# Forget-gate attention: where the next head's decay sums and six half projections stand among a head's eight iterations

## The reference, cut to what matters

```python
log_f = jax.nn.log_sigmoid(f_logit + b_f)
f_cum = jnp.cumsum(log_f, axis=1).transpose(0, 2, 1)
...
logits = jnp.einsum("bhqd,bhkd->bhqk", qi, k) * scale
logits = logits + fi[..., :, None] - f_cum[..., None, :]
logits = jnp.where(pi[:, None] >= kpos[None, :], logits, -jnp.inf)
probs = jax.nn.softmax(logits, axis=-1)
return jnp.einsum("bhqk,bhkd->bhqd", probs, v)
...
return o * jax.nn.silu(z)
```

## Time and profile before

| what | us |
|---|---|
| median of 3 runs (lowest, highest) | 3028.71 (3024.96, 3031.01) |
| profiled execution, its own time | 3029.29 |
| its span, first to last instruction | 3028.0 |
| PE busy | 2837.0 |
| ACT busy | 1349.0 |
| DVE busy | 1617.8 |
| POOL busy | 856.2 |

### The profile page before, as it was taken

How to read it: one execution, slowest core, us unless ns; L and a number is a source line. 1 busy time by engine, 2 the same in 40 slices (tenths; PEclk the granted TensorE clock), 3 DMA queues, 4 the chain that set the end, 5 groups by cost and what they waited for, 6 DMA issues and landing times.

```text
span 3028.0 us, 36823 instructions
## 1 busy us (share of the span) xinstructions
PE 2837.0 (94%) x14072; PEld 2328.6 (77%) x14072; DVE 1617.8 (53%) x2879; ACT 1349.0 (45%) x2400; POOL 856.2 (28%) x671
## 2 busy tenths in 40 slices
PE   7989989998999999999997999999999999989987
PEld 6777768776778888887774777778888888877876
DVE  5656674543288888886587676630002434342034
ACT  5656773434266666674434334451113334332122
POOL 1333341223255544542111221123221111103331
PEclk9999999999999999999998999999999999999999
DMA  3011111221100000002351110012211010101231
GB/s 126 29 39 32 39 70 53 78 86 35 34 10 14 10 10 10 10 28 84 101 163 71 46 35 22 15 51 68 70 49 42 22 35 29 28 15 56 70 111 69
DMA packets 54445, 148.81 MB, mean 49 GB/s; under 512 B 6144, under 2 KB 14976, under 8 KB 54272
## 3 DMA queue, kind: packets, MB, share of 16 engines
q1 hardware_dynamic: 54272, 146.46, 15.1%
HBM read 129.66 MB, written 16.78 MB: 48 GB/s over the span
## 4 chain that ended last, share of the span: by engine, by line
PE 81%; DVE 9%; ACT 6%; issue 3%; DMA 1%; POOL 1%; SPq 0%; DVEq 0%; ACTq 0%; POOLq 0%
PE ps L317 75%; PE ps L362 4%; PE ps L659 1%; ACT t L302 1%; PE ps L2380 1%; DVE t L1019 1%; DVE t L1564 0%; ACT t L698 0%; POOL t L308 0%; DVE t L2617 0%; DVE t L1841 0%; DMA t<-in_abias 0%; DVE t L2624 0%; DVE t L2714 0%; DVE t L1743 0%
## 5 line engine op out<-in xcount | busy, mean ns | idle before, releaser
L317 PE MATMUL ps<-t,t 128*128 128x512 f32 (+7 forms) x12184 | 2668.8, 378 | 149.8 <-DVE t L758 27.3
L317 PEld LDWEIGHTS ps<-t,t 128*128 128x128 f32 (+3 forms) x12184 | 2123.9, 188 | 626.9 <-issue 110.5
L308 POOL TENSOR_TENSOR t<-t,t 128x1024 fp32r<-128x1024 f32 (+2 forms) x171 | 358.9, 2099 | 1320.7 <-ACT t L302 1320.1
L302 ACT ACTIVATE t<-t 128x1024 fp32r<-128x1024 f32 (+2 forms) x205 | 186.9, 912 | 698.1 <-PE ps L317 696.3
L1620 POOL TENSOR_SCALAR t<-t,t 128x1024 f32<-128x1024 f32 x128 | 145.2, 1135 | 183.0 <-DVE t L1570 180.0
L362 PE MATMUL ps<-t,t 128*128 128x128 f32 x1176 | 160.5, 274 | 13.4 <-DVE t L1564 7.7
L1564 DVE TENSOR_TENSOR t<-ps,t 128x512 fp32r<-128x512 f32 x256 | 164.2, 681 | 15.7 <-ACT t L1481 13.9
L362 PEld LDWEIGHTS ps<-t,t 128*128 128x128 f32 x1176 | 132.0, 140 | 37.6 <-issue 26.4
L1577 DVE TENSOR_REDUCE t<-ps 128x1 f32<-128x1024 f32 x128 | 154.0, 1203 | 2.0 <-PE ps L317 1.9
L1481 ACT ACTIVATE t<-ps 128x512 fp32r<-128x512 f32 x256 | 140.2, 592 | 11.5 <-PE ps L362 7.4
L1489 ACT ACTIVATE t<-ps,t 128x1024 f32<-128x1024 f32 x128 | 142.7, 1115 | 1.9 <-DVE t L1577 1.5
(11 more groups left out here) (217 smaller groups left out, 2427.2 us busy)
## 6 DMA issues: line engine op xcount, KB each, us to landing
t<-in_wflat SPq DMA_DIRECT2D x156, 512.0 KB, 3.6
t<-in_wada SPq DMA_DIRECT2D x48, 256.0 KB, 3.4
t<-in_xT SPq DMA_DIRECT2D x16, 512.0 KB, 8.1
t<-in_wflat SPq DMA_DIRECT2D x32, 128.0 KB, 2.0
hd<-t SPq DMA_DIRECT2D x8, 512.0 KB, 3.1
t<-hd SPq DMA_DIRECT2D x8, 512.0 KB, 7.5
x2d<-t SPq DMA_DIRECT2D x8, 512.0 KB, 4.0
md<-t SPq DMA_DIRECT2D x16, 256.0 KB, 4.3
```

Of the source, the lines that this page charges most:

```text
L302: ac.activation(whi[i % 2][:, 0:n], raw[i % 2][:, 0:n], ACT.Copy).then_inc(*on.up(ac, "whi", i))
L308: e.tensor_tensor(wlo[i % 2][:, 0:n], raw[i % 2][:, 0:n], whi[i % 2][:, 0:n], ALU.subtract) \
L317: return pe.matmul(o, l, r, start=start, stop=stop)
```

## The change

It puts the two decay sums first in `parts` and the six half projections behind them, and adapts the three places that turn a step's number into a half. On all three engines the steps of iterations 0 to 7 are then sum 0, sum 1, Q0, Q1, K0, K1, V0, V1, in place of Q0, Q1, K0, K1, V0, V1, sum 0, sum 1. The banks of the iterations, the sizes and everything else stay. In head 0's preparation the order changes in the same way.

```diff
@@ stage_attn_c
-            parts = [(FQ, 0), (FQ, 1), (FK, 0), (FK, 1), (FV, 0), (FV, 1), None, None]
+
+            parts = [None, None, (FQ, 0), (FQ, 1), (FK, 0), (FK, 1), (FV, 0), (FV, 1)]
@@ head(h, s, b), the branch of the sums
-                    hf = s - 6
+                    hf = s
                     bank["f", h, hf] = b
                     wait_bank(b)
@@ head_dv(h, s)
-                if s < 2:
-                    on.wait_ge(dv, "fq_hi", h, s)
-                    dv.scalar_tensor_tensor(Qf[h % 2][1][:, half(s)], ps[:, bank[FQ[h], s], :], C_SCALE, Qf[h % 2][0][:, half(s)], ALU.mult, ALU.subtract) \
-                        .then_inc(*on.up(dv, "fq_lo", h, s))
-                elif s < 4:
-                    hf = s - 2
+                hf = s % 2
+                if s in (2, 3):
+                    on.wait_ge(dv, "fq_hi", h, hf)
+                    dv.scalar_tensor_tensor(Qf[h % 2][1][:, half(hf)], ps[:, bank[FQ[h], hf], :], C_SCALE, Qf[h % 2][0][:, half(hf)], ALU.mult, ALU.subtract) \
+                        .then_inc(*on.up(dv, "fq_lo", h, hf))
+                elif s in (4, 5):
                     on.wait_ge(dv, "fk_hi", h, hf)
```

## The result

| | before | changed |
|---|---|---|
| median of 9 runs, us | 3028.71 | 3045.36 |
| lowest, highest | 3024.2, 3036.49 | 3036.03, 3052.99 |
| profiled execution: its time, span | 3029.29, 3028.0 | 3036.03, 3034.7 |
| first copy of z (start of the stage) to the end of the span | 849.1 | 861.2 |

The ratio is 1.0048, 95% interval 1.0032 to 1.0064: slower, by about 14.5 us, with 9.7 and 19.4 at the ends of the interval. The forecast was 3040, within 3034 to 3048.

The account below looks back on a forecast made before the run. The prediction took PE, busy 94% of the span, as the bound, so only gaps on PE count. Its terms, 16.0 + 0.5 + 0.7 - 6.1 = +11.1 us, gave a forecast of 3040 us, range 3034 to 3048.

Parts of the forecast that it names:

- Term 1: After the last V half, the chain to iteration 1's value products outlasts PE's remaining work: 1.67 us lost per head change.
- term 2: Between the transposes of iterations 1 and 2, a 3.13 us chain against 2.13 of PE work: 1.00 us lost per head change.
- term 4: Old stalls at iteration 7 (0.50 us, seven heads) and iteration 0 (0.44 us, six heads) go away: 6.1 us saved.
- Term 3, the loop's start: At the loop's start the first sum waits for V's half in bank 7, losing 1.48 us instead of 0.80: +0.7.
- Term 3, the last head: At the change to the last head the value products' wait loses 2.61 us instead of 2.13: +0.5.
- The clock did not fall at the six head changes: Rival: the clock falls to 1.2 GHz at all six head changes, up to 1.75 us each, giving 3050 us; 12%.
- No change: Rival: half of each loss at the head changes is hidden, giving 3032 us; 8%.
- Faster: Rival: the narrow iterations' chains are hidden and only the saving of old stalls remains, giving 3022.6 us; 4%.
- V's second half behind the first in bank 7: At the wide end V's second half waits for bank 7: expected free; as rival, about 1 us a head, 3047; 2%.

Follow-up runs that it names:

- free_banks: The changed kernel with the steps of iterations 0 and 1 writing banks 1 and 3 instead of 7 and 1; 3041.68 us, ratio 1.0044 to the kernel before.
- late_copy: free_banks with ACT's weight cast and V copy of iteration 7 moved behind two instructions of the next iteration; 3032.49 us, ratio 1.0012 to the kernel before.
- one_sum: The changed kernel with only one sum in front: sum 0, Q0, Q1, K0, K1, V0, V1, sum 1, its banks kept; 3027.56 us, one run.
- spread: The changed kernel with free_banks' banks and order Q0, Q1, K0, sum 0, K1, sum 1, V0, V1; 3025.14 us, ratio 0.9990 to the kernel before.
- fill3: The changed kernel with free_banks' banks and order Q0, Q1, K0, sum 0, K1, V0, V1, sum 1; 3018.73 us, ratio 0.9979 to the kernel before.
- before_banks: The kernel before with one edit: the steps of iterations 0 and 1 write banks 1 and 3; 3021.67 us, one run.
- after_again: The changed kernel without any edit, timed again in a second series beside the kernel before; 3042.94 us, ratio 1.0041 to the kernel before.

## Why the prediction was right, and where it was not

- **Term 1 (1.67 us a head) and term 2 (1.00)**, less the 0.50 and 0.44 of term 4, gave +1.73 us a head; measured +1.71. The value products start 2457.70 - 2454.07 = 3.63 us after the first transpose, forecast 3.50 + 0.16 = 3.66. The eight transposes start 3.13 us after the seven, as in the earlier trace rows. free_banks, late_copy and one_sum show that the links are the ones named: bank 7 adds nothing, ACT's cast and V copy are 0.84 us of the chain, and a projection at iteration 1 removes term 2 whole.
- **Term 3, the loop's start, had the wrong sign.** The step that failed is "now V's half lies in bank 7 (the first head takes banks 4 to 7 in turn)". The turn does not begin at bank 4, because earlier stages take from the same rotation. The earlier trace rows said so: Q starts at 2298.39, and the copy of the first head's sums, 2297.12 + 2.16 = 2299.28, was then still going on (line below), so it was the first sum that lay in bank 7. In the changed kernel V's first half lies there, and PE sees no wait at the start. From the first copy of z to the first head change it is 1.4 us faster (167.17 to 165.76), of which 0.80 is this stall and 0.50 that of iteration 7; forecast was +0.7 - 0.5.

```profile
2297.12 2.16 ACT L2467 ACTIVATE t<-ps,t 128x128 f32<-128x128 f32 x8
```

- **Term 3, the last head, was too small.** Forecast +0.5, measured +2.5 (31.88 to 34.35 us between the six transposes of the last two heads). The wait grew as forecast, from 1.96 to 2.43 us. But the 18 value products behind it then took 2690.95 - 2687.32 = 3.63 us in place of 2.15:

```profile
2687.32 3.83 PE L317 MATMUL ps<-t,t 128*128 128x256 f32 x18 [2.43 <-DVE t L2488]
2690.95 0.97 PE L2381 MATMUL ps<-t,t 128*128 128x128 f32 x7
```

  The granted clock there fell to 1.2 GHz right after the longest wait; over 2680 to 2690 us it is 0.88 and over the next 10 us 0.84, where the earlier trace rows has 1.00 over the corresponding 12 us:

```profile
2680.00:2690.00 10.00, 7.57 (x41) 6.68 (x40) 2.60 (x7) 3.37 (x5) 2.35 (x1) 0.88 0.16 39
2690.00:2700.00 10.00, 6.36 (x41) 6.06 (x41) 4.64 (x13) 2.81 (x6) 0.00 (x0) 0.84 0.04 15
```

  The longer wait alone does not cost 2.5 us, though. The run spread has the same wait of 2.43 us and much the same slow value products behind it (3.61 us), but its last head takes 31.84 us, as in the kernel before. There the clock stayed up behind the wait of 1.88 us, and the 24 products took 2.87 us (2699.71 - 2696.84):

```profile
2686.57 3.77 PE L317 MATMUL ps<-t,t 128*128 128x256 f32 x18 [2.43 <-DVE t L2488]
2690.18 0.95 PE L2381 MATMUL ps<-t,t 128*128 128x128 f32 x7
...
2696.84 3.04 PE L317 MATMUL ps<-t,t 128*128 128x256 f32 x24 [1.88 <-DVE t L2488]
2699.71 0.30 PE L2381 MATMUL ps<-t,t 128*128 128x128 f32 x1
```

  In the changed kernel the same 24 took 4.36 us and in the kernel before 4.37. The granted clock over the whole last head is 0.89 before and in spread, and 0.85 in the changed kernel. An estimate from that: some 7 us of it ran at 1.2 GHz in the first two, some 10 in the last. So 0.5 us of the loss is the wait, as forecast, 1.5 stand in the slow value products, and the other 0.5 could not be placed; the failed part of the term is that it held nothing for the clock. Why the lower clock adds up in one order and not in the other stays open.

- **Behind the loop** 0.8 us more were lost (315.89 to 316.67 us from the last head's six transposes to the span's end), for which no term stood. They lie in the 365 matmuls behind PE's wait of 9 us; over the first 10 us of these the granted clock is 0.83 in the kernel before and 0.70 in the changed one. In the kernel before:

```profile
2921.76 87.66 PE L317 MATMUL ps<-t,t 128*128 128x512 f32 x365 [9.36 <-POOL t L2617]
```

and in the changed one:

```profile
2927.28 88.88 PE L317 MATMUL ps<-t,t 128*128 128x512 f32 x365 [8.97 <-POOL t L2618]
```

- **The sum.** Heads 10.3, start -1.4, last head 2.5, behind it 0.8 make, to rounding, the 12.1 us measured from z to the end. Forecast was 11.1. The heads, nearly all of it, were right for the stated reason; that the total is so close besides is luck, since the start came out 1.6 us too high and the last head and what follows 2.8 us too low.
- **The rivals.** The clock did not fall at the six head changes in either profile, whose gaps are at most 0.82 us, nor at those of free_banks with 1.48 us; it fell at the one with 2.4 us. "No change" needed half of each loss hidden, and 1.71 of 1.73 us came. "Faster" needed the value products free at 1.83 us: they came at 3.63 - 0.16 = 3.47. V's second half behind the first in bank 7 showed no wait. The Trainium skill (Perfetto Trace Analysis, Identifying the Most-Contended Engine) judges TensorE's headroom by the weight loads' busy share, beside the share of peak arithmetic. For an edit of order the trace does not bear this out: fill3 leaves the weight loads busy 322.59 of 375 us, and PE has no gap to give.
- **The size in the medians**, +16.7 by the two and +14.5 by the ratio, is above the 12.1 of the profile; the interval from 9.7 holds both, and the second series gave +12.4. The nine runs of either kernel scatter over 12 and 17 us, and how much of the difference between 12.1 and 14.5 is scatter is not shown.

## What to carry to other kernels

A large block of independent work is cover for a latency chain, and in a software pipeline the longest chain does not lie in the widest iteration: here the probabilities of the widest blocks are transposed, copied and split three iterations later, in the next head's narrowest iterations, so 3.6 and 3.1 us of chain fell where PE had the least else to do. Before moving such a block, lay the chain of the neighbouring engines (start to start, from rows) beside the work that is left over it, at its old and at its new place. And before freeing a buffer that a wait names, check that no other chain ends at the same instruction.

## What the runs showed of the hardware that was not expected

Executions of the same kernel differ by 10.7 us before the stage begins (first copy of z at 2173.5 and 2184.2 us) and by 0.2 us after it, so a trace compared from a fixed instruction on resolves what a median of nine runs does not. At the change to the last head the clock stayed at 2.4 GHz behind the shorter waits and fell to 1.2 GHz behind the longer one, in all nine profiles. In the five with a wait of 1.59 to 1.97 us (before, one_sum, before_banks, fill3, late_copy) the 18 value products behind it took 2.15 us; in the four with 2.43 us (changed, after_again, free_banks, spread) they took 3.6 us. No run set out to vary this wait alone, so that its length is the cause is only argued. Nor does its length alone decide: behind the later wait of 1.88 us in the same head the clock fell in eight of the nine profiles and stayed up in spread. That is why spread's last head takes 31.84 us and that of the other three with the 2.43 us wait 34.3 to 34.4.
